# The first expert of 32 run alone, its down weights loaded before the order of the experts is known

## The reference, cut to what matters

```python
def _moe(h, router_w, router_b, w_up, b_up, w_down, b_down):
    logits = (h @ router_w + router_b).astype(jnp.float32)
    top_vals, top_idx = lax.top_k(logits, TOP_K)
    gates = jax.nn.softmax(top_vals, axis=-1)
    ...                       # tokens sorted by expert, padded to blocks of 128
    def expert_block(args):
        xb, e = args
        u = xb @ w_up[e] + b_up[e]
        return _clamped_swiglu(u) @ w_down[e] + b_down[e]
    ...                       # each row times its gate, added to its token
```

## Time and profile before

| | us |
|---|---|
| median of three runs | 1397.94 |
| the profiled execution | 1400.33 |
| its span, first to last instruction | 1398.5 |
| PE busy in it | 1311.2 (94%) |
| DVE busy | 1185.3 (85%) |
| ACT busy | 1055.6 (75%) |
| POOL busy | 281.0 (20%) |
| DMA mean share of 16 engines, weights queue | 77.2% |

### The profile page before, as it was taken

The page is one execution under the profiler, slowest core; times in us unless marked ns, Lnnn a source line. Parts: engine busy times, 40 slices in busy tenths (PEclk is TensorE's granted clock), DMA queues, the critical chain, the costliest instruction groups (busy, mean ns, idle before and its releaser), DMA issues.

```text
span 1398.5 us, 18794 instructions
## 1 busy us (share of the span) xinstructions
PE 1311.2 (94%) x6287; PEld 1059.7 (76%) x6288; DVE 1185.3 (85%) x1064; ACT 1055.6 (75%) x900; POOL 281.0 (20%) x140
## 2 busy tenths in 40 slices
PE   6999989989998999999999999999999999999992
PEld 5888866678776878888788877778788878787771
DVE  5566645578998899999999999999999999999975
ACT  6454334336787898988889898989898888989873
POOL 0000001110165323322122121121122312212310
PEclk9999999989999999999999999999999999999996
DMA  8522153226999999999999999999999999999964
GB/s 243 143 61 76 46 199 163 94 103 252 406 337 408 371 411 412 409 414 397 420 400 416 405 420 403 398 402 414 416 405 408 407 413 406 421 404 408 399 248 140
DMA packets 71415, 457.92 MB, mean 327 GB/s; under 512 B 7371, under 2 KB 36203, under 8 KB 46737
## 3 DMA queue, kind: packets, MB, share of 16 engines
q1 hardware_dynamic: 64560, 438.13, 77.2%
q0 software_dynamic: 6816, 19.30, 5.8%
HBM read 443.35 MB, written 18.48 MB: 330 GB/s over the span
## 4 chain that ended last, share of the span: by engine, by line
PE 65%; DMA 16%; DVE 10%; issue 5%; ACT 3%; DVEq 0%; POOL 0%; SPq 0%; POOLq 0%; ACTq 0%
PE psum L1856 40%; DMA w_raw_pair<-w_up 11%; PE psum L1614 8%; DVE w_low L1258 5%; PE psum L1611 3%; DMA residual_rows<-y_rows,scatter_rows 3%; ACT w_high L777 2%; PE psum L1700 2%; PE psum L1748 2%; PE psum L1849 1%; PE psum L1839 1%; PE psum L1902 1%; DMA w_buf<-w_out 1%; PE psum L1724 1%; PE psum L1872 1%
## 5 line engine op out<-in xcount | busy, mean ns | idle before, releaser
L1258 DVE TENSOR_TENSOR w_low<-w_raw_pair,w_high 128x2048 fp32r<-128x2048 f32 x382 | 854.1, 2285 | 61.0 <-ACT w_high L777 60.1
L777 ACT ACTIVATE w_high<-w_raw_pair 128x2048 fp32r<-128x2048 f32 x384 | 717.8, 1911 | 117.2 <-DMA w_raw_pair<-w_up 45.6
L1856 PE MATMUL psum<-w_high,x_high 128*128 128x512 f32 x1040 | 286.3, 397 | 22.2 <-DVE x_high L1441 17.8
L1856 PE MATMUL psum<-w_low,x_high 128*128 128x512 f32 x1040 | 281.3, 392 | 0.0
L1856 PEld LDWEIGHTS psum<-w_high,x_high 128*128 128x128 f32 x1040 | 194.0, 190 | 71.1 <-DVE w_low L1258 27.4
L1856 PEld LDWEIGHTS psum<-w_low,x_high 128*128 128x128 f32 x1040 | 197.0, 189 | 42.2
L583 POOL DMA_INDIRECT residual_rows<-y_rows,scatter_rows x32 | 126.5, 3953 | 340.0 <-ACT y_rows L815 338.4
L1856 PE MATMUL psum<-w_high,a_high 128*128 128x512 f32 x496 | 156.2, 396 | 0.0
L1856 PE MATMUL psum<-w_low,a_high 128*128 128x512 f32 x496 | 154.2, 392 | 0.0
L1856 PE MATMUL psum<-w_high,x_low 128*128 128x512 f32 x512 | 141.1, 397 | 1.7 <-DVE w_low L1258 1.2
L1856 PEld LDWEIGHTS psum<-w_high,x_low 128*128 128x128 f32 x512 | 93.4, 188 | 26.8 <-issue 4.8
(11 more groups left out here) (306 smaller groups left out, 1451.4 us busy)
## 6 DMA issues: line engine op xcount, KB each, us to landing
w_raw_pair<-w_up SPq DMA_DIRECT2D x128, 2048.0 KB, 16.0
w_raw_pair<-w_down SPq DMA_DIRECT2D x64, 2048.0 KB, 14.9
w_in_raw<-w_in SPq DMA_DIRECT2D x28, 512.0 KB, 3.8
w_buf<-w_out SPq DMA_DIRECT2D x2, 2048.0 KB, 11.1
x_rows<-x SPq DMA_DIRECT2D x4, 512.0 KB, 5.4
x_rows<-x SPq DMA_DIRECT2D x1, 2048.0 KB, 18.8
residual_rows<-x_rows SPq DMA_DIRECT2D x4, 512.0 KB, 2.6
normed_rows<-h_rows SPq DMA_DIRECT2D x4, 512.0 KB, 2.6
```

Of the source, the lines that this page charges most:

```text
L777: act.activation(wh[:, q.slot(m, SPL), :], raw[q.slot(m, RAW)][:, :], ACT.Copy).then_inc(wh_ready, 1)
L1258: dve.tensor_tensor(wl[q.slot(m, RAW)][:, :], raw[q.slot(m, RAW)][:, :], wh[:, q.slot(m, SPL), :].bitcast(F32), ALU.subtract).then_inc(wl_ ...
L1856: ins = pe.matmul(o[:, j, :], x_part, w_part[:, j * 512:(j + 1) * 512], start=(first and n == 0), stop=(last and n == len(passes) - 1))
```

## The change

FIRST is now all 12 chunks of expert 0, SECOND the 8 up chunks of expert 1; from chunk 20 on the numbers are as before. SP loads expert 0's down part (two pairs, into slots 8 to 11) ahead of the last wait for the normed rows and of the wait for the order. PE runs down(0) behind the turns, then up(1), its fold and the biases of up(2), and then the loop as before. ACT, DVE and their waits are put into the order that belongs to this; ACT's first round of the loop is written out, since big_step(2) now begins with other waits. In the last small step the up fold moves from ahead of down(30) to behind its first chunk, with the copy on ACT and the activation behind it two to four places later. What is computed stays the same, and so does the number of matmuls, casts, splits and loads.

```diff
@@ -407,9 +407,11 @@
 
         CHUNKS = [("up", c) for c in range(UPC)] + [("down", c) for c in range(DNC)]
         FIRST = Chunks(0, 0, 0)
-        SECOND = Chunks(0, 0, UPC)
+        SECOND = Chunks(0, 0, NC)
         END = Chunks(0, 0, UPC + NC * (NE - 1))
 
+        THIRD = Chunks(0, 0, UPC + NC)
+        FOURTH = Chunks(0, 0, UPC + 2 * NC)
         BEFORE = Chunks(0, 0, UPC + NC * (NE - 3))
         LAST = Chunks(0, 0, UPC + NC * (NE - 2))
 
@@ -509,6 +511,10 @@
                 for n in range(2):
                     freed(sp, "x2", i, n)
                 sp.dma_start(accv[:, i, :], X[:, i, :]).then_inc(S("acc_out"), 16)
+                if i == TT - 1:
+
+                    for n in range(UPC, NC, 2):
+                        load_pair(FIRST, n, n, 0)
                 sp.wait_ge(S("h2_rows"), i + 1)
                 sp.dma_start(norv[:, i, :], H2[:, i, :]).then_inc(S(f"normed_out{i}"), 16)
 
@@ -517,7 +523,7 @@
 
             sp.wait_ge(ids_ready, 1)
             e1 = expert_at(1)
-            step(SECOND, e1, 0)
+            step(SECOND, e1, None)
             with sp.Fori(0, PAIRS) as i:
                 e_before, e_big, e_small = expert_at(i * 2 + 1), expert_at(i * 2 + 2), expert_at(i * 2 + 3)
                 step(big_chunks(i), e_big, e_before)
@@ -856,10 +862,8 @@
                         gated(p - 2, y_col, PH)
                         a_high(use_a(p - 1))
                         bias_row(BSD, of_place(p - 1), bsd_ready)
-                    if n == 9 and last:
+                    if n == 11 and last:
                         up_low_rows(p, q.count(UPC - 1, 1))
-                    if n == 11 and last:
-                        silu_half((p - 1) // 2)
                     cast(q, n, n)
 
             def router_half(i, n):
@@ -897,30 +901,44 @@
 
             act.activation(warm[:, 2:3], warm[:, 0:1], ACT.Silu).then_inc(S("tables"), 1)
             act.wait_ge(S("turn_values"), 1)
-            for n in range(SPL - 1, UPC):
+            for n in range(SPL - 1, NC):
                 cast(FIRST, n, n)
             act.wait_ge(ids_ready, 1)
-            for n in range(NC):
-                if n == 2:
-                    bias_row(BSU2, of_place(1), bsu_ready, PH)
-                if n == 5:
-                    act.wait_ge(chunk_used, FIRST.count(UPC - 1, 1))
-                    x_high(X1, PH)
-                    silu(0, FIRST.count(UPC - 1, 1))
+            bias_row(BSU2, of_place(1), bsu_ready, PH)
+            bias_row(BSD, of_expert(0), bsd_ready)
+            cast(SECOND, 0, 0)
+            act.wait_ge(chunk_used, FIRST.count(UPC - 1, 1))
+            x_high(X1, PH)
+            silu(0, FIRST.count(UPC - 1, 1))
+            a_high(use_a(0))
+            for n in range(1, UPC):
+                if n == 6:
+                    gated(0, 0)
+                cast(SECOND, n, n)
+
+            cast(THIRD, 0, 0)
+            up_low_rows(1, SECOND.count(UPC - 1, 1))
+            cast(THIRD, 1, 1)
+            silu_half(0)
+            x_high(use_x(2))
+            bias_row(BSU, of_place(2), bsu_ready)
+            for n in range(2, NC):
                 if n == 8:
-                    a_high(use_a(0))
-                    bias_row(BSD, of_expert(0), bsd_ready)
-                cast(SECOND, n, n)
-            with act.Fori(0, PAIRS) as i:
+                    a_high(use_a(1), PH)
+                    bias_row(BSD2, of_place(1), bsd_ready, PH)
+                cast(THIRD, n, n)
+            small_step(3, FOURTH, expert_at(1))
+            with act.Fori(1, PAIRS) as i:
                 big_step(i * 2 + 2, big_chunks(i), i, expert_at(i * 2))
                 small_step(i * 2 + 3, small_chunks(i), expert_at(i * 2 + 1))
             e28, e29, e30, e31 = (expert_at(n) for n in range(NE - 4, NE))
             big_step(NE - 2, BEFORE, PAIRS, e28)
             small_step(NE - 1, LAST, e29, True)
             cast(END, UPC, 0)
+            silu_half(PAIRS + 1)
+            cast(END, UPC + 1, 1)
             a_high(LAST_A, PH, xh)
             bias_row(BSD2, of_place(NE - 1), bsd_ready, PH)
-            cast(END, UPC + 1, 1)
             gated(NE - 2, e30)
             for n in range(UPC + 2, NC):
                 cast(END, n, n - UPC)
@@ -1474,7 +1492,7 @@
                         a_low_half(p - 1)
                     split(q, n)
 
-            def small_step(p, q, last=False):
+            def small_step(p, q):
                 for n in range(NC):
                     if n == 1:
                         swiglu(p - 1)
@@ -1482,8 +1500,6 @@
                         x_low_half(p)
                     if n == 8:
                         a_low(p - 1)
-                    if n == 11 and last:
-                        swiglu(p, PH)
                     split(q, n)
 
             order_experts()
@@ -1507,23 +1523,26 @@
             split(FIRST, 6)
             split(FIRST, 7)
             turn_sels()
-            for n in range(NC):
-                if n == 2:
-                    x_low_half(1)
-                    turn_rows()
-                    swiglu(0)
-                if n == 8:
-                    a_low(0)
+            for n in range(UPC, NC):
+                split(FIRST, n)
+            split(SECOND, 0)
+            x_low_half(1)
+            turn_rows()
+            swiglu(0)
+            a_low(0)
+            for n in range(1, UPC):
                 split(SECOND, n)
             further_blocks()
             with dve.Fori(0, PAIRS) as i:
                 big_step(i * 2 + 2, big_chunks(i))
                 small_step(i * 2 + 3, small_chunks(i))
             big_step(NE - 2, BEFORE)
-            small_step(NE - 1, LAST, True)
+            small_step(NE - 1, LAST)
             split(END, 0)
+            swiglu(NE - 1, PH)
+            split(END, 1)
             a_low_half(NE - 1, xh)
-            for n in range(1, DNC):
+            for n in range(2, DNC):
                 split(END, n)
             overflow_items()
             dve.wait_ge(S("blocks_known"), 1)
@@ -1950,20 +1969,14 @@
                 for c in range(UPC):
                     up_chunk_half(q, c)
                     if c == 1:
-                        if fold_before is not None:
-                            down_fold(p - 2, fold_before)
+                        down_fold(p - 2, fold_before)
                         a_transposed(p - 1, use_a(p - 1))
-                if fold_before is None:
-                    pe.wait_ge(turns_ready, 1)
-                    pe.wait_ge(S("turn_gates"), 1)
-                if last:
-                    up_fold(p, fold)
                 down(p - 1, use_a(p - 1))
                 for c in range(DNC):
                     down_chunk(q, UPC + c, c)
                     if c == 0 and not last:
                         x_transposed(p + 1, use_x(p + 1))
-                    if c == 1 and not last:
+                    if c == (0 if last else 1):
                         up_fold(p, fold)
                     if c == 2 and last:
                         a_transposed(p, LAST_A, PH)
@@ -1989,7 +2002,21 @@
                 if c == 5:
                     x_transposed(1, X1, PH)
             turns()
-            small_step(1, SECOND, 0, None)
+            a_transposed(0, use_a(0))
+            pe.wait_ge(turns_ready, 1)
+            pe.wait_ge(S("turn_gates"), 1)
+            down(0, use_a(0))
+            for c in range(DNC):
+                down_chunk(FIRST, UPC + c, c)
+                if c == 0:
+                    x_transposed(2, use_x(2))
+            down_bias(0)
+            pe.wait_ge(u_free, 1)
+            up(1)
+            for c in range(UPC):
+                up_chunk_half(SECOND, c)
+            up_fold(1, 0)
+            up_biases(2)
             with pe.Fori(0, PAIRS) as i:
                 big_step(i * 2 + 2, big_chunks(i))
                 small_step(i * 2 + 3, small_chunks(i), i + 1, i)
```

## The result

| | before | after |
|---|---|---|
| median | 1400.46 us | 1414.39 us (1413.7 to 1416.9, four runs) |
| ratio | | 1.0098, 95% interval 1.0079 to 1.0117 |
| profiled execution | 1400.33 us, span 1398.5 | 1413.7 us, span 1411.9 |
| mean granted clock | 0.979 | 0.975 |

13.7 us is the ratio times the median before; the medians differ by 13.9. The forecast was 1406 (8 us more) with a range of 1396 to 1413. The direction was right, the size was not: the result lies 1.4 us outside the range. Of the 8.4 us between 1406 and 1414.4, 2.5 are the base alone: the median before was 1397.94 in three runs when the forecast was made and is 1400.46 with a fourth. The rest is the forecast's own error in what the change costs.

The account below looks back on a forecast made before the run. The weight stream was taken to bound the long loop. PE's path, 17.5 - 6.8 - 2.9 = +7.8 us, chose +8 within the stream's +6.4 to +14.3: 1406 us from a median of 1397.94, range 1396 to 1413.

Parts of the forecast that it names:

- PE's chain at the start: From the turns to the end of chunk 20: new waits and half clock, up(2) 15.9 us later, together +17.5 us.
- The clock: Half clock on PE after each of the start's two new bubbles, priced at 2.5 us each.
- Rival (a): At the start, the clock does not fall in the two bubbles: PE's path +2.8 us, 1400.7 us; chance 0.30.
- The end: Last small step: later up fold saves 1.96 us waiting and 2.0 of half clock, costs 1.1: -2.9 us.
- The preload: Two pairs (10.3 us) loaded into the hole before 326 us; the queue then idles longer, about 355.5 to 373 us.
- Rival (b): Stream is the bound, stays fed from 326 us; preloaded pairs count in full: 13.2 us faster, 1384.7; chance 0.12.
- The gather: Gather of expert 4 in the loop no longer late, since scatter(0) starts at about 382 us: -6.8 us.
- the DMA path: Weight stream's sum: pair needing 22 used chunks leaves 17.2 us later; total between +6.4 and +14.3 us.
- the lost stream of 7.9 us: Old stream not full from 393 to 470 us: 3.5 + 4.4 us lost, which the new kernel might win back.
- PE's own sum: PE's path over start, gather and end: 17.5 - 6.8 - 2.9 = +7.8 us.
- the pair: Weight pair waiting for 22 used chunks, forecast to leave SP at 410.5 instead of 393.3 us, +17.2.
- Rival (c): Nothing of the DMA loss comes back and the gather is late: +14.3 us, 1412; chance 0.08.

Follow-up runs that it names:

- experiment 7: The changed kernel with identity matmuls filling PE's waits around expert 0's activation transposes and the up fold: 1409.32 us, ratio 1.0058 to before.
- experiment 1: The kernel before with only the end edit, the last up fold behind the first chunk of down(30): 1399.19 us, ratio 0.998.
- experiment 2: The changed kernel with the end edit taken back, so only the start part: 1415.16 us, ratio 1.0091 to before.
- experiment 3: The changed kernel with expert 0's two down pairs loaded behind the wait for the expert order: 1412.68 us, ratio 1.0074 to before.
- experiment 4: The kernel before, old order, with two up pairs of expert number 1 loaded ahead of the wait for the order: 1401.47 us, ratio 1.0003.
- experiment 11: experiment 1 with DVE's table of further blocks moved behind the loop's first round: 1399.17 us, ratio 0.9988 to before.
- experiment 6: The changed kernel with 32 identity matmuls on PE ahead of the transposes of x(4): 1415.64 us, ratio 1.0103 to before.
- experiment 5: The kernel before with the gather of expert 4 ahead of scatter(0) on POOL: 1401.8 us, ratio 1.0009.
- experiment 10: experiment 1 with the split of chunk 7 moved from DVE to POOL: 1404.76 us, ratio 1.003 to before.

## Why the prediction was right in its steps and wrong in its sum

**PE's chain at the start: right.** Forecast: waits of 6.9, 2.2 and 4.4 us, 2.0 for the transposes, up(2) 15.9 us later. Measured: 6.65, 2.58 and 3.88, plus 1.96 for the fold's copy (forecast as 2.0), 1.98 for the transposes, up(2) 17.1 later, of which 1.7 us lie upstream of any change (below).

**The clock: right in kind, about 1 us too dear.** Rival (a), bubbles without a half clock, fell by the rows at 361.94 and 404.39 (1.98 and 2.07 us for what takes 1.23 in experiment 7 and 1.19 in the earlier trace rows at the full clock) and by experiment 7. On PE's path the half clock costs 2.1 us behind each bubble in after, 4.2 together, where the forecast had 5: the transposes and the first chunk of down(0) (0.8 and 1.3 us longer than the same work in before), then the biases and the first chunks of up(2) (1.0 and 1.1). The Trainium skill, "TensorE: Matmul & The Clock Gate" (Part 1), says that the ramp is under 1% of a typical kernel's span and that a model should not be fitted to a count of slow matmuls. This agrees in size: 4.2 us are 0.3%. To leave the ramps out, as the forecast read it for rival (a), misleads here all the same, since the whole effect is 1%.

**The end: right.** Forecast -2.9; the traces give -2.4 to -2.5 between last mark and last split (the new wait is 1.33 us; the forecast had 1.1, where its own two offsets give 0.9). The times are too coarse to tell the size: -2.8 by the ratio of experiment 1 and -1.6 by its medians, and nothing clear between experiment 2 and after.

**The preload: its dry queue was foreseen.** Rival (b), 1384.7, fell: slot 8 came free only with down(0), and experiments 3 and 4 show that a preload is worth nothing in either order. On "Perfetto Trace Analysis" (Optimization Strategy) of the Trainium skill, by which interleaving regimes may gain: the trace agrees, PE's busy time from 325 to 377 us fell from 49.0 to 41.06 when the two experts were no longer interleaved.

**The gather: the place was right, the worth wrong.** The wait of 4.33 us is gone (456.79, no wait), and the scatter starts at 383.84. The second mark indeed comes only 10.3 us late, 7.1 less than the first. But the third is at 14.5 again. The -6.8 us was a gain on PE alone, and PE is not what is late in the loop: experiment 11 has the same 7.1 us in the old order and no better time, and experiment 6 puts 7.3 us of work back, at the same place, for 0.7 to 1.3 us.

**The step that failed: the DMA path.** The forecast gave its two ends, +6.4 if the lost stream of 7.9 us from 393 to 470 comes back and +14.3 if none does, and then took "the low part of this, where PE's own sum lies". There was no row for that choice. That all or much of it comes back takes for granted that the new stream is full once the pair has left, and this is the term that was put at nothing: what the new order loses itself up to 470 us. Of the 7.9 us only 2 to 3 came back. The first part came: 393 to 404 us runs at 410 instead of 279 GB/s, 3.5 us, as worked out. But the pair leaves at 411.4, and from there the window reads

```profile
411.00:470.00 59.00, 58.56 (x268) 47.66 (x267) 58.05 (x32) 53.49 (x39) 10.25 (x7) 1.00 0.97 372
```

Against 409 GB/s that is (409 - 372) x 59 = 2.2 MB or 5.3 us of lost stream behind the pair, so 7.9 - 5.3 = 2.6 us came back. Over the same 77 us in both kernels, 393 to 470, the rates are 377 and 367 GB/s, (377 - 367) x 77 = 0.8 MB or 1.9 us. Up to 415 us the queue is dry, because the same bubble that delays up(2) also keeps the slots; why it runs at 318 to 377 GB/s from there to 440 us stays open. The sum with the measured term is 17.2 - 2.6 - 2.9 = +11.7 us (12.4 with the 1.9); the spans differ by 13.4, of which 1.7 lie upstream: 11.7. Rival (c) had the right size (+14.3) for half the right reason: nothing much of the stream came back, but the gather was not late.

The two paths were also put together in the wrong manner: PE's sum of +7.8 was used to choose inside the stream's +6.4 to +14.3. In this loop, which the stream bounds, the later of the two decided, and the saving on PE was used up within two or three rounds (7.1 us at the second mark in after and in experiment 11, 2.8 and 2.6 left at the third).

## What to carry to other kernels

In a loop that a weight stream bounds, work out a change before it in bytes: how many megabytes the queue has moved by the loop's first full stretch, before and after. The difference by the loop's rate was nearly all that arrived at the loop's end here (14 of 15.9 us), and a stall of PE during which the queue ran on counted for next to nothing. Loading ahead into a hole is worth something only if the ring's slots come free soon enough afterwards, so look at the share behind the hole, not in it. An independent second expert beside the first one's activation is what covers that activation; without it each serial hand-over was paid twice here, in waiting and in clock.

## What the runs showed of the hardware

**The same short wait costs the clock in some executions and not in others.** PE waits for the output projection's weights at 206 us in both kernels, in code that the change does not touch (before, then after):

```profile
205.67 3.67 PE L1700 MATMUL psum<-w_buf,gate_T 128*128 128x512 f32 x8 [2.48 <-DMA w_buf<-w_out]
```

```profile
205.87 5.17 PE L1719 MATMUL psum<-w_buf,gate_T 128*128 128x512 f32 x8 [2.41 <-DMA w_buf<-w_out]
```

3.67 us in one, 5.17 in the other: the granted clock from 206 to 211 us is 1.00 and 0.71. That is 1.5 of the 1.7 us that the profiled after is late before anything changed. Of the six profiled executions with the old start two have the slow form of this wait (experiments 5 and 11, 5.37 us behind waits of 2.23 and 2.37), three the fast one (before and experiments 1 and 10, 3.67 us behind 2.33 to 2.48); in the sixth (experiment 4) PE does not wait for these weights, and the clock fell at 197 us, behind another wait of 1.79 us. All seven with the new start have the slow form, behind 2.08 to 2.41 us. So the length of the wait does not tell the two apart. Whether that is chance or the layout of the program stays open; if it belongs to the new start, 1.5 us of the 13.7 are this and not the order. "TensorE: Matmul & The Clock Gate" of the Trainium skill (Part 1) says that the count of slow matmuls at the start of a kernel varies from run to run of one kernel. These rows, from the middle of different kernels with the same code up to there, show the like.

**DVE and POOL took turns, they did not share.** In experiment 10 POOL's split starts at 340.11 while DVE is in one of its splits (until 341.9), and takes 6.26 us; DVE's next operation starts at 341.82 and ends at 348.5. If POOL begins only when DVE's split is over, it needs 6.26 - 1.8 = 4.5 us; DVE then begins at 346.4 and needs 2.15. The kernel before has a POOL subtraction of the full size in 4.49 us, which agrees. There the roles are the other way round: POOL starts first, and an operation of DVE on four columns, which took 0.23 us at 301.10, takes 4.38 us and ends when POOL's does, at 309.3 us:

```profile
304.76 4.49 POOL L562 TENSOR_TENSOR w_low<-w_raw_pair,w_high 128x2048 fp32r<-128x2048 f32 x1 [29.77 <-ACT w_high L777]
304.90 4.38 DVE L1250 TENSOR_SCALAR small<-small 128x4 f32<-128x4 f32 x1
```

"SBUF — State Buffer" of the Trainium skill (SBUF: two separate sides) has a lock on a shared pair of ports that the loser waits for in full; these durations agree with it.
